# A twelve-stage transformer stack on one core: another order of the attention scores and values between the eight units of the hybrid mixer

## The reference

```
s_s = einsum('bqgrd,bqgmd->bqgrm', qi, ks) * scale - slopes * dist
p_s = masked_softmax(s_s, dist_s >= 0)
o_s = einsum('bqgrm,bqgmd->bqgrd', p_s, vs)
(the same with kw, vw for o_w)
o = gs[..., 0:1] * o_c + gs[..., 1:2] * o_s + gs[..., 2:3] * o_w
```

## Time and profile before

| what | value |
|---|---|
| median of three runs | 1811.67 us (1811.58 to 1812.54) |
| the profiled execution, whole | 1811.9 us |
| its span, first to last instruction | 1810.1 us |
| TensorE busy | 1798.3 us, 99% of the span |
| VectorE busy | 1312.2 us, 72% |
| ScalarE busy | 1052.0 us, 58% |
| GpSimd busy | 237.4 us, 13% |
| granted TensorE clock, mean | 0.999 of full |

### The profile page before, as it was taken

One profiled execution on the slowest core, in us unless ns is written; L12 is line 12 of the kernel. 1 busy time (PEld: TensorE's weight loads), 2 busy tenths in 40 slices (PEclk: granted clock), 3 DMA queues, 4 the chain that ended last, 5 costly groups with the idle time before them and its releaser, 6 DMA issues.

```text
span 1810.1 us, 26703 instructions
## 1 busy us (share of the span) xinstructions
PE 1798.3 (99%) x10311; PEld 1546.9 (85%) x10311; DVE 1312.2 (72%) x1714; ACT 1052.0 (58%) x1524; POOL 237.4 (13%) x259
## 2 busy tenths in 40 slices
PE   9999999999999999999999999999999999999998
PEld 7888899788888888889987888889888889888887
DVE  7767778876766776677688677667887667797665
ACT  7555546755655565455476665555775555675443
POOL 2010122110000011003021000002100111301110
PEclk9999999999999999999999999999999999999999
DMA  9686663462765567666345456555447664645662
GB/s 337 219 297 208 172 191 106 140 221 93 252 193 183 163 219 254 228 169 220 118 139 198 136 189 210 188 177 186 154 146 226 190 198 157 230 136 187 196 191 71
DMA packets 226815, 338.96 MB, mean 187 GB/s; under 512 B 22566, under 2 KB 170176, under 8 KB 226432
## 3 DMA queue, kind: packets, MB, share of 16 engines
q1 hardware_dynamic: 219200, 308.11, 52.5%
q0 software_dynamic: 7488, 29.14, 4.8%
HBM read 336.18 MB, written 1.05 MB: 186 GB/s over the span
## 4 chain that ended last, share of the span: by engine, by line
PE 95%; DVE 2%; DMA 1%; ACT 1%; SPq 0%; issue 0%; POOL 0%; DVEq 0%; ACTq 0%
PE ps L1809 92%; PE ps L1814 3%; DVE wlo L1195 1%; DMA raw<-ffn_w_down 1%; DVE xn L1195 1%; ACT whi L742 0%; DVE xs L1203 0%; DVE ahl L1195 0%; SPq L537 0%; POOL region L564 0%; SPq L549 0%; ACT xn L742 0%; DVE region L1195 0%; SPq L541 0%; ACT ahl L742 0%
## 5 line engine op out<-in xcount | busy, mean ns | idle before, releaser
L1195 DVE TENSOR_TENSOR wlo<-raw,whi 128x1024 fp32r<-128x1024 f32 (+2 forms) x452 | 560.7, 1241 | 172.3 <-ACT whi L742 137.2
L742 ACT ACTIVATE whi<-raw 128x1024 fp32r<-128x1024 f32 (+2 forms) x452 | 475.7, 1052 | 74.7 <-PE ps L1809 28.2
L1809 PE MATMUL ps<-ahl,whi 128*128 128x512 f32 (+1 forms) x1824 | 402.7, 355 | 0.6 <-ACT whi L742 0.6
L1809 PEld LDWEIGHTS ps<-ahl,whi 128*128 128x128 f32 x1824 | 320.9, 189 | 47.4 <-ACT whi L742 1.0
L742 ACT ACTIVATE region<-ps 128x512 f32<-128x512 f32 (+2 forms) x268 | 155.9, 582 | 272.9 <-PE ps L1809 220.2
L1809 PE MATMUL ps<-whi,ahl 128*128 128x512 f32 (+2 forms) x944 | 299.0, 385 | 0.5 <-ACT whi L742 0.5
L1809 PE MATMUL ps<-ahl,wlo 128*128 128x256 f32 x1520 | 244.4, 283 | 0.0
L1809 PEld LDWEIGHTS ps<-ahl,wlo 128*128 128x128 f32 x1520 | 214.8, 191 | 6.4
L1809 PEld LDWEIGHTS ps<-whi,ahl 128*128 128x128 f32 x944 | 174.2, 188 | 34.7 <-ACT region L742 1.6
L1195 DVE TENSOR_TENSOR mlo<-raw,mhi 128x1024 fp32r<-128x1024 f32 (+2 forms) x132 | 163.3, 1237 | 44.8 <-ACT mhi L742 35.4
L1809 PE MATMUL ps<-whi,hhi 128*128 128x512 f32 x472 | 185.7, 393 | 0.0
(11 more groups left out here) (176 smaller groups left out, 2349.1 us busy)
## 6 DMA issues: line engine op xcount, KB each, us to landing
raw<-w_ff SPq DMA_DIRECT2D x64, 1024.0 KB, 5.4
raw<-ffn_w_down SPq DMA_DIRECT2D x44, 1024.0 KB, 5.0
raw<-ffn_w_up SPq DMA_DIRECT2D x40, 1024.0 KB, 5.7
raw<-ffn_w_gate SPq DMA_DIRECT2D x39, 1024.0 KB, 5.3
raw<-w_in SPq DMA_DIRECT2D x34, 1024.0 KB, 5.4
raw<-w_out SPq DMA_DIRECT2D x16, 1024.0 KB, 4.9
raw<-xa_wk SPq DMA_DIRECT2D x8, 1024.0 KB, 5.1
raw<-xa_wv SPq DMA_DIRECT2D x8, 1024.0 KB, 5.0
```

The costliest lines, as they stand in the source:

```text
L742: e.activation(o, i, f, **kw).then_inc(*act.did(*names))
L1195: e.tensor_tensor(o, a, b, op).then_inc(*dve.did(*names))
L1809: m = e.matmul(o, l, r, start=start, stop=stop)
```

## The change

The scores of units 0 and 1 are made together, unit 1's in bank 2 (`score_head`). On TensorE the scores of units 2 and 3 move from the start of u = 1 to u = 0 ahead of the turning of unit 0, those of 4 and 5 from u = 3 to u = 2, those of 6 and 7 from u = 5 to u = 4; the values of pairs 0 to 2 move from the end of u = 1, 3, 5 to directly ahead of these scores (pair 2 stands alone at u = 6); the turning back moves one unit later. VectorE's shifts of units 3 and 5 and its `value` move with them, `fin` of row block 0 moves from u = 5 to u = 6 on VectorE and from u = 4 to u = 5 on ScalarE, and `coef` gets a second buffer, taken in turn.

```diff
-        coef = st[:, 32:40]
+        coefs = [st[:, 32:40], SM[:, 72:80]]
...
+        def score_head(u, i):
+            m, g, br = HUNITS[u]
+            w = 128 * (m + 1)
+            if u == 1:
+                return PS[:, 2, i * 128:(i + 1) * 128]
+            return PS[:, 4 + 2 * g + i // 2, (i % 2) * 256:(i % 2) * 256 + w]
...
 (ScalarE, hybrid)
                 for u, (m, g, br) in enumerate(HUNITS):
+                    memory_piece(s, 2 * u)
                     if u in (2, 4, 6):
                         values(u // 2 - 1)
-                    memory_piece(s, 2 * u)
...
-                    if u == 4:
+                    if u == 5:
                         fin(s, l, 0)
...
 (VectorE, hybrid)
                     if u == 0:
                         take(s, "g_r", 1)
-                    if u < 7:
+                    if u < 7 and u not in (2, 4):
                         shift(u + 1)
                     if u == 3:
                         for h in range(2):
                             halves(s + 0.5, h, 1, h)
+                    if u == 6:
+                        fin_var(s, l, 0)
                     if u < 7:
                         maximum(u + 1)
                     if u == 3:
                         take(s, *HSPLIT[2], 0)
-                    if u in (2, 4, 6):
+                    if u in (3, 5, 7):
                         value(u // 2 - 1)
                     if m:
                         q.wait_ge(*pe.at("h_turned", l, u, 1))
                         cp(hPT[u % 2][:, 512:1024], PS[:, 1, :], ("h_pt", l, u))
+                    if u == 6:
+                        fin(s, l, 0)
...
                     weight(u)
+                    if u in (1, 3):
+                        shift(u + 2)
                     if u == 5:
-                        fin_var(s, l, 0)
                         split_to(number[s, "wv", 3], halves=1)
-                        fin(s, l, 0)
...
 (TensorE, hybrid)
                     for u in units:
                         if u >= 2:
                             q.wait_ge(*dve.at("h_shift", l, u - 2, 3))
-                        elif u == 1:
+                        if u == 3:
                             q.wait_ge(*dve.at("ret_centred", l))
...
-                scores(0)
+                scores(0, 1)
...
                 for u, (m, g, br) in enumerate(HUNITS):
                     o = u % 2
-                    if u in (1, 3, 5):
-                        scores(u + 1, u + 2)
                     if u == 3:
                         q.wait_ge(*act.at("memory", l, 5))
                         blocks(s + 0.5, 1, 1, 1)
                     memory_piece(s, 2 * u)
+                    if u in (3, 5, 7):
+                        turn_back(u // 2 - 1)
+                    if u in (2, 4, 6):
+                        values(u // 2 - 1)
+                    if u in (0, 2, 4):
+                        scores(u + 2, u + 3)
                     q.wait_ge(*act.at("h_exp", l, u, 3))
                     if u == 0:
                         q.wait_ge(*dve.at("g_r", l, 0))
-                    if u in (2, 4, 6):
-                        turn_back(u // 2 - 1)
...
-                    if u == 0:
-                        scores(1)
                     memory_piece(s, 2 * u + 1)
-                    if o:
-                        values(u // 2)
+                    if u == 7:
+                        values(3)
```

More of the change, by code:

```diff
@@ L1498, in cmp_coef @@
                 def cmp_coef(m):
-                    tt(coef, den, gates[:, m, :].rearrange("p (h b) -> p h b", b=3)[:, :, 0], ALU.mult)
+                    tt(coefs[0], den, gates[:, m, :].rearrange("p (h b) -> p h b", b=3)[:, :, 0], ALU.mult)
                 def cmp_turn(m):
@@ L1508, in cmp_out @@
                     for g in range(2):
-                        tt(om[:, 4 * g:4 * g + 4, :], PS[:, 0:4, g * 64:(g + 1) * 64], bc(coef[:, 4 * g:4 * g + 4], 64), ALU.mult,
+                        tt(om[:, 4 * g:4 * g + 4, :], PS[:, 0:4, g * 64:(g + 1) * 64], bc(coefs[0][:, 4 * g:4 * g + 4], 64), ALU.mult,
                            ("cmp_out", l, m, g))
@@ L1545, in shift @@
                     m, g, br = HUNITS[u]
-                    w, b = 128 * (m + 1), 4 + 2 * (u % 2)
+                    w = 128 * (m + 1)
                     al = ALIBI[:, 0:128] if m == 0 else ALIBI[:, 128:384]
@@ L1551, in shift @@
                     for i in range(4):
-                        stt(hP[u % 2][:, i, 0:w], al, 8.0 * SLOPES[4 * g + i], PS[:, b + i // 2, (i % 2) * 256:(i % 2) * 256 + w],
-                            ALU.mult, ALU.add, ("h_shift", l, u, i))
+                        stt(hP[u % 2][:, i, 0:w], al, 8.0 * SLOPES[4 * g + i], score_head(u, i), ALU.mult, ALU.add,
+                            ("h_shift", l, u, i))
                 def maximum(u):
@@ L1567, in weight @@
                     rcp(den[:, o:o + 4], den[:, o:o + 4])
-                    tt(coef[:, o:o + 4], den[:, o:o + 4], gm[:, 4 * g:4 * g + 4, 1 + br], ALU.mult)
+                    tt(coefs[u // 2 % 2][:, o:o + 4], den[:, o:o + 4], gm[:, 4 * g:4 * g + 4, 1 + br], ALU.mult)
                 def value(j):
@@ L1575, in value @@
                     tt(tmp.rearrange("p (g i d) -> p i g d", g=2, i=4), PS[:, 2, :].rearrange("p (i g d) -> p i g d", i=4, g=2),
-                       bc(coef.rearrange("p (g i) -> p i g", g=2), 64), ALU.mult, ("h_out", l, j))
+                       bc(coefs[j % 2].rearrange("p (g i) -> p i g", g=2), 64), ALU.mult, ("h_out", l, j))
                 head(0)
@@ L2226, in scores @@
                             m, g, br = HUNITS[u]
-                            w, b = 128 * (m + 1), 4 + 2 * g
-                            mm(PS[:, b + i // 2, (i % 2) * 256:(i % 2) * 256 + w], qT[g * 64:g * 64 + 64, i, m * 128:(m + 1) * 128],
+                            w = 128 * (m + 1)
+                            mm(score_head(u, i), qT[g * 64:g * 64 + 64, i, m * 128:(m + 1) * 128],
                                kvv[g * 64:g * 64 + 64, 2 * br, 0:w], True, True, *([("h_scores", l, u)] if i == 3 else []))
```

## The result

| | before | after |
|---|---|---|
| median of five runs | 1812.04 us (1811.58 to 1812.80) | 1826.45 us (1825.20 to 1827.91) |
| ratio | | 1.0082, 95% interval 1.0071 to 1.0093 |
| the profiled execution, whole | 1811.9 us | 1827.91 us |
| its span | 1810.1 us | 1826.1 us |
| TensorE busy | 1798.3 us | 1801.6 us |

The change made the kernel slower by 14.4 us, 0.8%. The direction was forecast; the size, +9.5, was not, and the median lies 0.45 us above the upper end of the stated range, 1826. The profiled execution is the slowest of the five; the first row of the page and the waits of TensorE answer to the earlier trace rows.

The account below looks back on a forecast made before the run. TensorE, busy 99% of the span, was taken to bound the kernel. Gains and waits summed to +4.74 us a layer, twice +9.5 on 1811.9, forecasting 1821.4 us, range 1816.5 to 1826.

Parts of the forecast that it names:

- 1 joined scores: Scores of units 0 and 1 made together on TensorE, the second half riding free: a gain of 1.28 us a layer.
- 2 merged stretches: Values and scores adjoining for pairs 0 and 1 save a change of array shape: gain 0.38 us a layer.
- 3 long wait: Scores of units 2 and 3, moved earlier, wait for VectorE's shift of unit 1: a loss of 4.4 us a layer.
- rival A: Waits as forecast, and TensorE's clock falls in the long one: 1822.9 us for one layer, up to 1824.9 for both; 33%.
- 4 pieces 10, 12: Two pieces lose the cover for ScalarE's copies of pieces 9 and 11: 0.9 us each, 1.8 a layer lost.
- 5 blocks, piece 8: Turning of blocks at u = 3 waits for piece 5's copy, piece 8 for a VectorE split: 0.2 us each.
- 6 turning back: The wait of the turning back behind piece 8 for ScalarE's copy of the values goes: 0.2 us gained.
- 7 row block 0, scores 6 and 7: Later root nearly covered, 0.6 us left; shift of unit 5 ends about 1 us before its scores ask: no cost.
- Rival C: Scores find the shift done and pieces 10 and 12 find bank 3 empty; only gains stay: 1808.2 us, 5%.

Follow-up runs that it names:

- e3: The kernel before with only the scores of units 0 and 1 made together, unit 1 in bank 2: 1812.07 us, ratio 1.0004.
- e2: The changed kernel with 32 unused matmuls filling the wait ahead of the scores of units 2 and 3: 1822.27 us.
- e7: The changed kernel with 18 unused matmuls ahead of the scores of units 2 and 3: 1825.11, 1823.52, 1825.73 and 1822.19 us.
- e4: The changed kernel with VectorE's shift of unit 1 ahead of the split of wk 1, all waits kept: 1817.08 us, ratio 1.0031.
- e11: The changed kernel with the scores of units 2 and 3 back at the start of u = 1: 1817.30 us, ratio 1.0032.
- e6: e1 with turning back and pair 2 values moved ahead as cover, and VectorE's shifts of units 3, 5 and piece 8's split earlier: 1813.80 us.
- e1: The changed kernel without the wait of unit 3's scores for the shift of unit 1: 1817.28 us, ratio 1.0031.
- e12: e9 with ScalarE's two copies of turned blocks at u = 2 ahead of the exponentials of unit 3: 1812.15 us, ratio 1.0003.
- e9: e6 with ScalarE's copy of piece 5 ahead of unit 3's exponentials, and row block 0 squared and scaled at u = 5 again: 1813.62 us.
- e10: e3 with VectorE's shift of unit 1 ahead of the split of wk 1: 1811.81 us, ratio 1.0002.
- e8: The changed kernel with 9 unused matmuls ahead of the scores of units 2 and 3: 1825.03, 1824.26, 1823.75 and 1823.61 us.

## Why the prediction was right in direction and wrong in size

By its own steps, in the first pass, from the distances of starts in the profiled execution:

| step | predicted, us a layer | measured |
|---|---|---|
| 1 joined scores | -1.28 | -1.28 (TensorE's lead in e3) |
| 2 merged stretches | -0.38 | about -0.4 |
| 3 long wait | +4.4 | +4.33 |
| rival A, slow clock | not in the sum | +2.31 |
| 4 pieces 10, 12 | +1.8 | +0.85, +1.12 |
| 5 blocks, piece 8 | +0.4 | +0.20, +0.29 |
| 6 turning back | -0.2 | -0.2 |
| 7 row block 0, scores 6 and 7 | 0 | +0.21, +0.13 |
| sum | +4.74 | +7.56; the pass as a whole +7.59 |

The pass as a whole is the time from the first scores to the output projection, 75.78 us before and 83.37 after; in e2, at full clock, it is 81.05, which is 2.32 less. The two passes account for 14.9 of the 16.0 us between the two profiled executions, and most of the rest is the 1.0 us at 29 us, which stands in no changed stage.

**The step that failed is the slow clock: the sum put it at nothing, and rival A, which held it, priced it too low.** The measured cost is 2.3 us a layer. The fall was named, with its place, and set aside or priced wrongly in two ways. First, I judged that a gap ending at 4.4 us might escape a fall seen 2.9 us behind an end; it came after 2.5 us in the profiled execution, and even an idle time of 2.2 us draws it in some runs (e7). The mean clock of all five runs, 0.995 to 0.997, shows that it fell in each. The main case should have held it. Second, its price was read off the start of the span, where the slow work lasts over 3 us, so 1.5 to 1.75 us a layer. Here the low level lasted 6.8 us, 5.1 of them with work on the array. The two passes of the profiled execution paid 2.31 and 2.34 us: 1811.9 + 9.5 + 4.65 = 1826.0, and with the 1.0 us at 29 us 1827.0, where the execution took 1827.91. The 0.9 left is the same that e2 shows, which tests the sum without the clock: 1822.27 measured against 1821.4. It lies in the short waits, 0.17, 0.09 and 0.34 us a layer above the terms of steps 4, 5 and 7. The upper end of the range, 1826, was built on the same short slow stretch: A reached 1824.9 by its own price. (The forecast's own range has a slip too: its terms add 0.8 upward, to 1822.2, or 1823.8 with the smaller waits, and not 1823.)

Step 3 was right in cause and size: e4 moves the shift ahead of the split and e11 the scores behind it, and they cut the wait to 0.87 and 1.07 us. Step 4 was right in size at piece 10; at piece 12 the copy would have held TensorE for all but 0.3 us, but VectorE's split came later still. Step 7 left 0.6 us at row block 0, and the row shows 0.21 lost. Step 2 can now be read. Values and scores of units 4 and 5 in one stretch:

```profile
310.92 3.01 PE L1823 MATMUL ps<-region 128*64 128x512 f32 x20
313.86 0.65 PE L1828 MATMUL ps<-cs,region 128*128 128x128 f32 x4
```

From 310.92 to 313.86 are 2.94 us, just 1.01 and 1.93 as each took alone before (301.87 to 302.88 and 327.14 to 329.07); in e6 the scores' start has a row of its own, at 304.64, 1.01 behind the values'. So the values cost as much before 64-row tiles as before the undivided array. Values of twice the length take 1.87 (335.68 to 337.55 before), 0.86 more, so about 0.15 of the 1.01 does not depend on the length, and it is paid at the change inside too. What is saved is one way in and one way out beside the pieces, 0.09 and 0.10 us. The Trainium skill, "TensorEngine Tiling (Array Packing)", section Key Properties, says that a change of tiling mode drains TensorE; the trace agrees, with the 0.15 us paid at the change inside.

What the prediction did not see at all is that a gain on TensorE in this loop is kept only as long as no wait takes it back. In the changed kernel the 1.28 us of joining are kept, as the sum of the table shows, since the long wait gives VectorE time. In the kernel before, e3 shows them lost to the next wait. And e1 has 8.6 us less between piece 0 and the scores of units 2 and 3 than e2, both at full clock, and is only 5.0 faster: the other 3.6 came back as later waits. Rival C's 1808.2 asked for all waits to go. No run here got there; the nearest, e12, still has 1.86 us of short waits in the first pass and stands at 1812.15. That the chain of scores, shift, maximum, exponentials and turning on VectorE and ScalarE is hardly a microsecond behind TensorE fits e3, e9 and e10, where a gain or a wait taken away was followed by waits of 0.9 to 1.3 us behind it; that no order of the two engines could do better is not shown.

## What to carry to other kernels

Where an instruction's releaser is done only 0.3 us before the instruction starts, moving the instruction earlier buys idle time; look first for what stands ahead of the releaser on the other engine. An idle time of TensorE has to be priced with the clock behind it. Here waits of up to 1.4 us left it at full, idle times of 2.2 us drew it down in some runs, and one of 4.3 us in every run, at about half as much again as the wait itself. A busy share of 99% does not say that work taken off the engine is time taken off the kernel: try the gain alone before building on it.

## What the runs showed of the hardware that was not expected

The granted clock can fall after the array is at work again: in e7 at 294.5, 0.7 us behind the end of an idle time of 2.2 us. Whether it falls, and by the mean clocks how long it stays down, differs between runs of one kernel. The low level lasted 3.4 us in e7 and e8 (293.5 to 297.0 in the latter) and 6.8 us in the changed kernel, and the changed kernel's runs spread over 2.7 us where those of the same kernel without idle time spread over 0.15. In the Trainium skill, "TensorE: Matmul & The Clock Gate", Part 1, idleness brings the slow state back; for the changed kernel the trace agrees, with 2.5 us from the last matmul to the fall.
